# Eight large experts of a two-block transformer: split products on the whole array against unsplit products on four 32-column tiles

## The chip, the core and the metric

The program runs on one core of a Trainium2 chip. The metric is the device time of one execution, in microseconds; the median of three runs is given. The engines are PE (matrix multiply, TensorE), DVE (VectorE), ACT (ScalarE), POOL (GpSimd) and SP, which issues the transfers from memory. PE reads from the on-chip memory of 128 partitions and writes to eight banks of 128 x 512 fp32 accumulators (`psum`).

## The reference

The program computes two transformer blocks on 256 tokens with D = 1024. Two layers of the first block end in a layer of 32 small experts (hidden width 256). The last layer of the second block ends in eight large experts with a hidden width of 2816, and each token goes to two of them. All arithmetic is fp32. Only the last stage matters here:

```python
def swiglu(h, w_gate, w_up, w_down):
    a = jnp.einsum("bsd,df->bsf", h, w_gate)
    u = jnp.einsum("bsd,df->bsf", h, w_up)
    return jnp.einsum("bsf,fd->bsd", jax.nn.silu(a) * u, w_down)

def moe_swiglu(h, router_w, w_gate, w_up, w_down):
    logits = jnp.einsum("bsd,de->bse", h, router_w).astype(jnp.float32)
    top_v, top_i = lax.top_k(logits, TOP_K)
    top_w = jax.nn.softmax(top_v, axis=-1)
    gates = jnp.sum(jax.nn.one_hot(top_i, N_EXPERTS, dtype=jnp.float32) * top_w[..., None], axis=-2)
    y = jnp.zeros(h.shape, jnp.float32)
    for e in range(N_EXPERTS):
        y = y + gates[..., e:e + 1] * swiglu(h, w_gate[e], w_up[e], w_down[e]).astype(jnp.float32)
    return y.astype(h.dtype)
```

On the inputs of the reference the eight experts get 69, 57, 40, 70, 76, 67, 75 and 58 tokens. The kernel computes an expert only for its own tokens, gathered side by side, and reads each weight once.

## The kernel before

**Slots.** `sparse_experts` gathers the tokens by expert into `xg` (1024 rows as 8 k-blocks of 128, one column for each slot). An expert with at most 128 tokens takes the short path, which works on a window of 128 slots from the expert's offset; one with more takes the general path over 256 slots. Each engine reads the expert's count into a register and branches (`by_width`, L2683 and L2684).

**Weights.** An expert has 3 x 11 tiles of 1 MB of weights. SP brings them (128 partitions x 8 KB) into a ring of nine, `weight_ring`, in the order in which PE wants them. A tile is refilled when PE has counted it as used. `SplitExpert` has 33 tiles for an expert and skips 3 places of the ring, so that each expert starts at the same place.

**Split products.** Every weight tile is split into two fp32r parts: ACT copies it to a rounded high part (L2068, `high`), DVE subtracts that from the tile for the low part (L2073, `low`). ACT's copy waits until PE has used the tile that had the buffer before. PE then computes high x high, low x high and high x low (`three_products`, L137 to L139), three matmuls of which each passes 512 weight columns (256 in the last step) through the array, with 128 slots as its stationary operand. The array is used whole, 128 rows x 128 columns.

**Steps.** The hidden width is worked in six steps, five of 512 and one of 256. For each step PE computes gate and up (`first`), ACT takes the Silu of gate (`squash`), DVE multiplies it with up (`combine`), PE turns the result by transposes (`turn`, L2015), ACT and DVE split the turned rows again (L2115, L2119, L2136, L2141), and PE computes the step's share of the down projection (`third`). The turn of a step stands in the middle of the next step's gate, so that ACT and DVE have their time. After the last step the result's rows are copied from two banks by ACT (L2125) and DVE (L2148), turned by PE (L2056) and written to `outT` by DVE (L2152). The first half is copied while PE works at the second half of the last down tile.

**The small experts** (`SmallExperts`, L2317 gate and up, L2348 down, L2338 and L2357 transposes) are another class that the change leaves alone. They use unsplit fp32 products on 64 slots in two column tiles of 64, so that two matmuls share the array; they stand in a loop of several experts a turn, whose general path lies behind each expert and is jumped over by a branch (L2302). An fp32 product is recorded as two loads and two matmuls. Their weights come in rows of 8 KB.

**Order.** Nothing schedules: each engine's instructions stand in the order of the code, SP's loads too, and waits on semaphores tie them together. The eight experts are written out one after the other; the general path is a loop in between.

## Time and profile before

| | |
|---|---|
| median of 3 runs | 2376.32 us (2370.53, 2376.32, 2376.93) |
| the profiled execution | 2376.97 us, its span 2375.2 us |
| PE busy | 2193.2 us, 92% of the span |
| DVE busy | 1452.3 us, 61% |
| ACT busy | 1179.4 us, 50% |
| read from memory | 605.11 MB, 255 GB/s over the span |
| the eight large experts | 1576.7 to 2351.0 us, in the span |
| granted clock of PE | 0.9 or more of full in all 40 slices |

Times within the trace count from the start of the span. The profile lists an instruction's start and duration; matmuls are pipelined, so each lasts longer than the distance to the next, and it is the distance that counts. "idle before <-releaser" is how long the engine stood before an instruction and what it then got. PEq or PEldq is PE's sequencer, which reads the instructions and takes the branches; "issue" is time for which the profile shows no other reason.

### The profile page before, as it was taken

How to read it: one execution, taken by the hardware profiler on the slowest of the kernel's cores; microseconds unless marked ns; L12 is line 12 of the kernel's file. 1: busy time of each engine (PE TensorE's matmuls, PEld its weight loads, DVE VectorE, ACT ScalarE, POOL GpSimd, SP SyncE). 2: the span in 40 equal slices, each digit the busy share in tenths (PEclk: the TensorE clock that was granted, in tenths of full speed). 3: DMA queues.
4: the chain of work that ended last, by engine and by line, in shares of the span. 5: the costliest groups of instructions: out<-in, count | busy, mean ns of one | idle time of the engine just before them, and what ended most of it. 6: DMA issues, size and time to landing. Idle time of an engine off the chain costs nothing.

```text
span 2375.2 us, 35807 instructions
## 1 busy us (share of the span) xinstructions
PE 2193.2 (92%) x13160; PEld 1772.4 (75%) x13160; DVE 1452.3 (61%) x1811; ACT 1179.4 (50%) x1463; POOL 70.2 (3%) x122
## 2 busy tenths in 40 slices
PE   7898988998998889898999989899999999999997
PEld 6774545976654459787998888778788887888886
DVE  5541113565311137964566698468888888888886
ACT  4432222363222234544433455357777777777675
POOL 0100000101000002000000200000000000000000
PEclk9999999999999999999999999999999999999999
DMA  7339998702499976242554633338999999999992
GB/s 261 130 137 419 419 419 298 220 34 92 173 418 419 419 270 184 90 160 89 183 190 144 184 125 125 125 123 319 385 334 389 346 338 390 334 388 349 337 395 107
DMA packets 253801, 609.28 MB, mean 257 GB/s; under 512 B 11216, under 2 KB 103200, under 8 KB 229008
## 3 DMA queue, kind: packets, MB, share of 16 engines
q1 hardware_dynamic: 247776, 590.84, 67.1%
q0 software_dynamic: 5248, 13.25, 2.5%
q8 instruction: 159, 2.61, 0.4%
q10 hardware_dynamic: 560, 2.10, 0.2%
q14 instruction: 58, 0.48, 0.1%
HBM read 605.11 MB, written 1.05 MB: 255 GB/s over the span
## 4 chain that ended last, share of the span: by engine, by line
PE 70%; DVE 12%; DMA 9%; ACT 4%; issue 3%; DVEq 1%; ACTq 0%; SPq 0%; POOLq 0%
PE psum L137 16%; PE psum L139 16%; PE psum L138 16%; DMA weight_ring<-in_moe_w_up_dram 8%; PE psum L2317 7%; PE psum L2348 2%; DVE weight_ring_rounded L116 2%; DVE h_cf L3257 1%; PE psum L936 1%; ACT scores L970 1%; PE psum L2838 1%; ACT weights_high_rounded L2068 1%; PE psum L2357 1%; PE psum L922 1%; PE psum L2015 1%
## 5 line engine op out<-in xcount | busy, mean ns | idle before, releaser
L2073 DVE TENSOR_TENSOR weight_ring_rounded<-weight_ring,weights_high_rounded 128x2048 fp32r<-128x2048 f32 x264 | 603.8, 2291 | 100.0 <-ACT weights_high_rounded L2068 98.9
L2068 ACT ACTIVATE weights_high_rounded<-weight_ring 128x2048 fp32r<-128x2048 f32 x264 | 504.9, 1916 | 149.7 <-PE psum L139 133.5
L2317 PE MATMUL psum<-weight_ring,scores 128*64 128x256 f32 x2048 | 261.3, 397 | 54.0 <-DMA weight_ring<-in_moe_w_up_dram 27.3
L137 PE MATMUL psum<-weights_high_rounded,scores_rounded 128*128 128x512 f32 (+1 forms) x768 | 291.4, 379 | 7.8 <-issue 4.1
L139 PE MATMUL psum<-weights_high_rounded,scores_rounded 128*128 128x512 f32 (+1 forms) x768 | 287.3, 374 | 0.0
L138 PE MATMUL psum<-weight_ring_rounded,scores_rounded 128*128 128x512 f32 (+1 forms) x768 | 286.6, 373 | 0.0
L2317 PEld LDWEIGHTS psum<-weight_ring,scores 128*64 128x64 f32 x2048 | 151.8, 141 | 164.0 <-issue 117.5
L139 PE MATMUL psum<-weights_high_rounded,xT_rounded 128*128 128x512 f32 (+3 forms) x688 | 259.0, 376 | 0.0
L2447 DVE COPY e_outT<-psum 128x512 f32 x64 | 44.3, 692 | 300.2 <-PE psum L2357 300.2
L137 PE MATMUL psum<-xT_high_rounded,weights_high_rounded 128*128 128x256 f32 x768 | 218.0, 284 | 2.2 <-DVE xT_rounded L369 1.4
L139 PE MATMUL psum<-xT_high_rounded,weight_ring_rounded 128*128 128x256 f32 x768 | 217.1, 283 | 0.0
L116 DVE TENSOR_TENSOR weight_ring_rounded<-weight_ring,weights_high_rounded 128x2048 fp32r<-128x2048 f32 (+3 forms) x76 | 159.7, 2113 | 64.9 <-ACT weights_high_rounded L112 64.4
L138 PE MATMUL psum<-xT_rounded,weights_high_rounded 128*128 128x256 f32 x672 | 189.1, 281 | 0.0
L137 PEld LDWEIGHTS psum<-weights_high_rounded,scores_rounded 128*128 128x128 f32 x768 | 145.4, 189 | 35.9 <-DVE weight_ring_rounded L2073 5.9
L139 PEld LDWEIGHTS psum<-weights_high_rounded,scores_rounded 128*128 128x128 f32 x768 | 145.1, 189 | 25.9
L138 PEld LDWEIGHTS psum<-weight_ring_rounded,scores_rounded 128*128 128x128 f32 x768 | 145.4, 189 | 24.9
L112 ACT ACTIVATE weights_high_rounded<-weight_ring 128x2048 fp32r<-128x2048 f32 (+3 forms) x76 | 133.4, 1767 | 48.1 <-PE psum L139 41.3
L139 PEld LDWEIGHTS psum<-weights_high_rounded,xT_rounded 128*128 128x128 f32 x688 | 131.4, 191 | 24.6
L137 PEld LDWEIGHTS psum<-xT_high_rounded,weights_high_rounded 128*128 128x128 f32 x768 | 144.9, 189 | 3.6 <-DVE xT_rounded L369 1.6
L139 PEld LDWEIGHTS psum<-xT_high_rounded,weight_ring_rounded 128*128 128x128 f32 x768 | 144.5, 188 | 0.0
L137 PE MATMUL psum<-weights_high_rounded,xT_rounded 128*128 128x512 f32 x352 | 139.8, 397 | 0.0
L138 PE MATMUL psum<-weight_ring_rounded,xT_rounded 128*128 128x512 f32 x352 | 138.8, 394 | 0.0
(581 smaller groups left out, 3521.0 us busy)
## 6 DMA issues: line engine op xcount, KB each, us to landing
weight_ring<-in_moe_w_gate_dram SPq DMA_DIRECT2D x152, 1024.0 KB, 9.5
weight_ring<-in_moe_w_up_dram SPq DMA_DIRECT2D x152, 1024.0 KB, 10.1
weight_ring<-in_moe_w_down_dram SPq DMA_DIRECT2D x152, 1024.0 KB, 10.3
weight_ring<-in_w_in_dram SPq DMA_DIRECT2D x20, 1024.0 KB, 8.3
weight_ring<-in_ffn_w_gate_dram SPq DMA_DIRECT2D x11, 1024.0 KB, 5.2
weight_ring<-in_ffn_w_up_dram SPq DMA_DIRECT2D x11, 1024.0 KB, 5.3
weight_ring<-in_ffn_w_down_dram SPq DMA_DIRECT2D x11, 1024.0 KB, 4.9
weight_ring<-in_w_out_dram SPq DMA_DIRECT2D x8, 1024.0 KB, 5.0
```

What stands on the lines that cost most here:

```text
L112: self.ring.nc.scalar.activation(self.high, self.whole, ACT.Copy).then_inc(self.ring.high_ready, 1)
L116: self.ring.nc.vector.tensor_tensor(self.low, self.whole, self.high.bitcast(F32), ALU.subtract).then_inc(self.ring.split_ready, 1)
L137: nc.tensor.matmul(out, lh, rh, start=start, stop=False)
L138: nc.tensor.matmul(out, lh, rl, start=False, stop=False)
L139: return nc.tensor.matmul(out, ll, rh, start=False, stop=stop)
L922: last = nc.tensor.transpose(c.psum[:, 4 + g % 2, a * P:(a + 1) * P], S[:, u % 4, place(i), s * P:(s + 1) * P], c.ident[:, :])
L936: last = nc.tensor.matmul(c.psum[:, 6 + u % 2, at:at + P], PT[g % PTS][:, a * P:(a + 1) * P], wide, start=(s == 0), stop=(s == kts[j] - 1))
L2068: self.c.nc.scalar.activation(ring.high(self.s0 + q, 1, SLOT), ring.view(self.p0 + q, 1, SLOT), ACT.Copy).then_inc(ring.high_ready, 1)
L2073: self.c.nc.vector.tensor_tensor(ring.low(self.p0 + q, 1, SLOT), ring.view(self.p0 + q, 1, SLOT), ring.high(self.s0 + q, 1, SLOT).bitcast( ...
L2317: last = self.c.nc.tensor.matmul(psum[at:at + W, x % 2, 0:CH], self.x[:, x % 2, k, :], w[:, k, :], start=(k == 0), stop=(k == k1 - 1), ski ...
L2348: last = nc.tensor.matmul(psum[h * W:(h + 1) * W, 4 + x % 2, :], self.hidden[:, m, :], wt[:, m, h * 512:(h + 1) * 512], start=(m == 0), st ...
L2447: nc.vector.tensor_copy(self.outT[:, :, bass.ds(o, W)].rearrange("p (h j) s -> p j h s", h=2), c.psum[:, 6 + y % 2, :].rearrange("p (j h s ...
```

## The change

`LargeExperts` takes the place of `SplitExpert`. What it does:

- The short path works on 96 slots and is taken up to 96 tokens.
- The hidden width is worked in three steps of 1024, 1024 and 768.
- The weights are not split. A k-block's product (`by_quarters`) puts 32 slots at a time as stationary operand into a tile of 32 columns of the array. The tiles at columns 0, 32 and 64 take slots 0 to 31, 32 to 63 and 64 to 95 and pass the first `main` weight columns (768, or 640 in the last step); the tile at column 96 takes the remaining 256 (or 128) columns for the three groups of slots one after the other, into the same banks on the partitions 96 to 127. Matmuls have at most 512 columns.
- Gate and up come in 4 tiles a step with rows of 4 KB (3 KB in the last step), down in 4, 4 and 3 tiles, with rows of 8 KB in the first two steps, where two hidden rows that follow each other lie side by side. That is 35 tiles an expert, one place of the ring skipped.
- ACT does the window's copy, Silu, the copy of the turned rows and half of the result's; DVE the product and the other half, and three copies to `outT`. The result's rows are turned in the middle of the next expert's first gate.
- The general path (`wide_tensor`, `wide_scalar`, `wide_vector`) reads the weight tiles where they are, with two row groups of 128 slots, and is written out and not a loop.
- The slots' weights are summed in bank 5 and not 3, and DVE clears `rows` once.

The core of the diff, without the unused general path, signals and bookkeeping:

```diff
-class SplitExpert:
...
-                    last = three_products(nc, psum[:, bank + j % 2, 0:cols], (self.xh[:, x, :], self.xl[:, x, :]),
-                                          (high[:, k, :], low[:, k, :]), x == 0, x == KD - 1)
...
-        self.c.nc.scalar.activation(ring.high(self.s0 + q, 1, SLOT), ring.view(self.p0 + q, 1, SLOT), ACT.Copy).then_inc(ring.high_ready, 1)
...
-        self.c.nc.vector.tensor_tensor(ring.low(self.p0 + q, 1, SLOT), ring.view(self.p0 + q, 1, SLOT),
-                                       ring.high(self.s0 + q, 1, SLOT).bitcast(F32), ALU.subtract).then_inc(ring.split_ready, 1)
...
+class LargeExperts:
...
+    W = 96
+    STEPS = ((0, 1024, 768), (1024, 1024, 768), (2048, 768, 640))
+    TILES = 35
...
+    def by_quarters(self, slots, w, bank, main, start, stop):
+
+
+        nc, psum = self.c.nc, self.c.psum
+        rest = w.shape[1] - main
+        for c0, c1 in ((0, 512), (512, main)):
+            for q in range(3):
+                last = nc.tensor.matmul(psum[32 * q:32 * q + 32, bank + c0 // 512, 0:c1 - c0], slots(q), w[:, c0:c1],
+                                        start=start, stop=stop, skip_group_check=True)
+            for q in range(3):
+                if c0 <= q * rest < c0 + 512:
+                    at = q * rest - c0
+                    last = nc.tensor.matmul(psum[96:P, bank + c0 // 512, at:at + rest], slots(q, True), w[:, main:],
+                                            start=start and at == 0, stop=stop, skip_group_check=True)
+        return last
+
+    def first(self, pe, e, name, j, bank, half=None):
+
+        _, width, main = self.STEPS[j]
+        for a in range(4):
+            at = self.tile(e, name, a)
+            self.landed(pe, at, 0)
+            w = self.c.ring.view(at, 2, width)
+            for k in (2 * a, 2 * a + 1):
+                if k == KD // 2 and half is not None:
+                    half()
+                x = self.x[:, e % 2, k, :]
+                last = self.by_quarters(lambda q, rest=False: x[:, 32 * q:32 * q + 32], w[:, k - 2 * a, :], bank, main, k == 0, k == KD - 1)
+            last.then_inc(self.c.ring.used, 1)
...
+    def turn(self, pe, e, j):
+        pe.wait_ge(*self.of(self.rows_made, e, j))
+        if j > 0:
+            pe.wait_ge(*self.of(self.hidden_ready, e, j - 1))
+        elif e > 0:
+            pe.wait_ge(*self.of(self.written, e - 1))
+        for b, rows in self.blocks(j):
+            last = self.c.nc.tensor.transpose(self.c.psum[:, 6 + b // 4, b % 4 * P:(b % 4 + 1) * P], rows, self.c.ident[:, :])
+        last.then_inc(self.turned.sem, 2 if j == 2 else 1)
+
+    def third(self, pe, e, j, spare=0, between=None):
+        pe.wait_ge(*self.of(self.hidden_ready, e, j))
+        hidden = self.hidden[(3 * e + j) % 2].rearrange("p (b s) -> p b s", s=P)
+        tiles = self.parts[f"down{j}"]
+        for a in range(len(tiles)):
+            at = self.tile(e, f"down{j}", a)
+            self.landed(pe, at, 0)
+            w = self.c.ring.view(at, 2, D)
+            for m in range(2):
+                kept = (a == 3) if j < 2 else (a == 2 and m == 1)
+
+                def slots(q, rest=False):
+                    if kept:
+                        return hidden[:, 2 * q + m if j < 2 else q, 96:P]
+                    return hidden[:, 2 * a + m, 32 * q:32 * q + 32]
+                last = self.by_quarters(slots, w[:, m, :], 4, 768, j == 0 and a == 0 and m == 0, j == 2 and a == 2 and m == 1)
+            last.then_inc(self.c.ring.used, 1 + (spare if a == len(tiles) - 1 else 0))
+            if between and a == 0:
+                between()
+
+    def turn_rows(self, pe, e):
+        pe.wait_ge(*self.of(self.rows_act, e))
+        pe.wait_ge(*self.of(self.rows_dve, e))
+        for b in range(6):
+            last = self.c.nc.tensor.transpose(self.c.psum[:, 6 + b // 4, b % 4 * P:(b % 4 + 1) * P], self.rows[:, b * P:(b + 1) * P], self.c.ident[:, :])
+        last.then_inc(self.rows_turned.sem, 1)
+
+    def narrow_tensor(self, pe, e, spare):
+        pe.wait_ge(*self.of(self.windowed, e))
+        if e > 0:
+            pe.wait_ge(*self.of(self.squash_done, e - 1, 2))
+        self.first(pe, e, "gate0", 0, 0, (lambda: self.turn_rows(pe, e - 1)) if e > 0 else None)
+        if e > 0:
+            pe.wait_ge(*self.of(self.rows_made, e - 1, 2))
+        self.first(pe, e, "up0", 0, 2)
+        pe.wait_ge(*self.of(self.squash_done, e, 0))
+        self.first(pe, e, "gate1", 1, 0, lambda: self.turn(pe, e, 0))
+        self.third(pe, e, 0)
+        self.first(pe, e, "up1", 1, 2)
+        pe.wait_ge(*self.of(self.squash_done, e, 1))
+        self.first(pe, e, "gate2", 2, 0, lambda: self.turn(pe, e, 1))
+        self.first(pe, e, "up2", 2, 2)
+        self.third(pe, e, 1, 0, lambda: self.turn(pe, e, 2))
+        self.third(pe, e, 2, spare)
+
+    def narrow_scalar(self, act, e):
+        copy, psum = self.c.nc.scalar.activation, self.c.psum
+        act.drain().then_inc(self.wide_windowed.sem, 1)
+        for j, (_, _, main) in enumerate(self.STEPS):
+            s = 3 * e + j
+            self.done(act, e, f"gate{j}")
+            if s > 0:
+                act.wait_ge(*self.of(self.rows_made, (s - 1) // 3, (s - 1) % 3))
+            copy(self.squashed[:, 0:main], psum[:, 0:2, :].rearrange("p b n -> p (b n)")[:, 0:main], ACT.Silu).then_inc(self.squash_done.sem, 1)
+            act.wait_ge(*self.of(self.turned, e, j))
+            if s > 1:
+                self.done(act, (s - 2) // 3, f"down{(s - 2) % 3}")
+            copy(self.hidden[s % 2][:, 0:main], psum[:, 6:8, :].rearrange("p b n -> p (b n)")[:, 0:main],
+                 ACT.Copy).then_inc(self.hidden_ready.sem, 2 if j == 2 else 1)
+        self.done(act, e, "down2")
+        copy(self.rows[:, 0:512], psum[:, 4, :], ACT.Copy).then_inc(self.rows_act.sem, 1)
+
+    def narrow_vector(self, dve, e, o):
+        nc, psum = self.c.nc, self.c.psum
+        for j, (_, _, main) in enumerate(self.STEPS):
+            s = 3 * e + j
+            self.done(dve, e, f"up{j}")
+            dve.wait_ge(*self.of(self.squash_done, e, j))
+            if s > 0:
+                dve.wait_ge(self.turned.sem, self.of(self.turned, (s - 1) // 3, (s - 1) % 3)[1])
+            nc.vector.tensor_tensor(self.hidden_rows[:, 0:main], self.squashed[:, 0:main], psum[:, 2:4, :].rearrange("p b n -> p (b n)")[:, 0:main],
+                                    ALU.mult).then_inc(self.rows_made.sem, 1)
+        self.done(dve, e, "down2")
+        nc.vector.tensor_copy(self.rows[:, 512:], psum[:, 5, 0:256]).then_inc(self.rows_dve.sem, 1)
+        made = psum[:, 6:8, :].rearrange("p b n -> p (b n)")[:, 0:768]
+        dve.wait_ge(*self.of(self.rows_turned, e))
+        nc.vector.tensor_copy(self.outT[:, 0:6, bass.ds(o, self.W)], made.rearrange("p (k s) -> p k s", k=6)[:, :, 0:self.W])
+        for m in range(2):
+            last = nc.vector.tensor_copy(self.outT[:, 6 + m, bass.ds(o, self.W)].rearrange("p (g s) -> p g s", g=3),
+                                         made.rearrange("p (g m s) -> p m g s", g=3, m=2)[:, m, :, self.W:])
+        last.then_inc(self.written.sem, 1)
...
+    def tensor(self, pe, spare):
+        following = self.load_count(pe, 0)
+        for e in range(self.n):
+            count = following
+            if e + 1 < self.n:
+                following = self.load_count(pe, e + 1)
+            self.by_width(pe, count, lambda: self.narrow_tensor(pe, e, spare), lambda: self.wide_tensor(pe, e, spare))
+        self.turn_rows(pe, self.n - 1)
+
...
-        way = SplitExpert(c, p0, per, chunks, xg, squashed, hidden, outT, landed, used)
...
+        way = LargeExperts(c, p0, n, per, xg, outT, landed, used, cnt_i, off_i)
```

How PE's instructions stand at the start of the first large expert, before. `weight_ring_rounded` are the low parts, `weights_high_rounded` the high parts, `scores_rounded` the window of slots:

```order
L2684 COMPARE_AND_BRANCH
L137 MATMUL psum<-weights_high_rounded,scores_rounded 128x512
L138 MATMUL psum<-weight_ring_rounded,scores_rounded 128x512
L139 MATMUL psum<-weights_high_rounded,scores_rounded 128x512
L137 MATMUL psum<-weights_high_rounded,scores_rounded 128x512
L138 MATMUL psum<-weight_ring_rounded,scores_rounded 128x512
L139 MATMUL psum<-weights_high_rounded,scores_rounded 128x512
```

And now; here `weights_high` is the window of 96 slots, and the shape is that of the output, 32 partitions by columns:

```order
L2216 COMPARE_AND_BRANCH
L2231 MATMUL psum<-weight_ring,weights_high 32x512 x3
L2236 MATMUL psum<-weight_ring,weights_high 32x256 x2
L2231 MATMUL psum<-weight_ring,weights_high 32x256 x3
L2236 MATMUL psum<-weight_ring,weights_high 32x256
L2231 MATMUL psum<-weight_ring,weights_high 32x512 x3
L2236 MATMUL psum<-weight_ring,weights_high 32x256 x2
```

Where three matmuls of the whole array passed 512 columns, nine on 32 columns each now pass 768 columns over each of four tiles, and every fp32 one is a pair in the trace.

At the end of an expert, PE before: the result's transposes, the jump, the general path in a loop, the next expert's count and branch:

```order
L2056 MATMUL psum<-ident,scores 128x128 x8
L2684 UNCONDITIONAL_BRANCH
L2161 UNCONDITIONAL_BRANCH
L2161 ISA
L2165 MATMUL psum<-scores,xT 128x256 x16
L2169 MATMUL psum<-xT_high,scores 128x256 x8
L2161 REGISTER_ALU
L2161 COMPARE_AND_BRANCH
L2686 UNCONDITIONAL_BRANCH
L2683 TENSOR_LOAD e_cnt_i
L2683 ISA x2
L2684 COMPARE_AND_BRANCH
```

The short path ends at `L2684 UNCONDITIONAL_BRANCH`; what lies between it and `L2683 TENSOR_LOAD` isn't executed. And now, on PE at the same place, the jump and the start of the general path:

```order
L2231 MATMUL psum<-weight_ring,xT_high 32x256 x3
L2236 MATMUL psum<-weight_ring,xT_high 32x256
L2216 UNCONDITIONAL_BRANCH
L2363 MATMUL psum<-weight_ring,scores 128x512 x64
L2370 MATMUL psum<-ident,xT 128x128 x16
L2363 MATMUL psum<-weight_ring,scores 128x512 x32
```

The last down products stand right before the jump, with no transposes between. The general path's end and the next expert's start on PE:

```order
L2370 MATMUL psum<-ident,xT 128x128 x12
L2385 MATMUL psum<-weight_ring,xT_high 128x512 x32
L2385 MATMUL psum<-weight_ring,scores 128x512 x24
L2370 MATMUL psum<-ident,xT 128x128 x16
L2218 UNCONDITIONAL_BRANCH
L2213 TENSOR_LOAD e_cnt_i
L2213 ISA x2
L2216 COMPARE_AND_BRANCH
L2231 MATMUL psum<-weight_ring,weights_high 32x512 x3
```

Between the jump (`L2216 UNCONDITIONAL_BRANCH`) and the next expert's count (`L2213 TENSOR_LOAD`) lie some 1,240 instructions of PE, where there were some 100; the result's transposes moved into the next expert.

## Rows read from the trace of the kernel before

**Rows 1.** The page's first line.

```profile
span 2375.2 us, 35807 instructions
```

**Rows 2.** Line L2152: duration min/median/max in ns, first and last start.

```profile
L2152 DVE COPY f_outT<-psum x8: 1217/1218/1226, 1676.3 to 2351.0; 128x1024 f32 x8
```

**Rows 3.** Busy time in stretches: start:end length, each engine (x instructions), granted clock, DMA.

```profile
1676.30:1772.70 96.40, 94.26 (x447) 77.85 (x446) 83.49 (x49) 71.20 (x48) 0.00 (x0) 1.00 0.97 356
1772.70:1869.10 96.40, 95.43 (x453) 79.05 (x452) 85.03 (x49) 68.69 (x47) 0.00 (x0) 1.00 0.98 362
```

**Rows 4.** Waits, 1676:2351: total us, times, longest us.

```profile
ACT weights_high_rounded L2068 <- PE psum L139: 111.8, 166, 2.3
...
PE psum L137 <- DVE weight_ring_rounded L2073: 3.7, 4, 1.2
PE psum L137 <- issue: 3.5, 6, 0.6
PE psum L2056 <- DVE scores L2148: 2.7, 7, 0.4
```

**Rows 5.** Timeline, 2344:2352: start, duration, instruction, xcount.

```profile
2344.36 0.39 PE L137 MATMUL psum<-weights_high_rounded,xT_rounded 128*128 128x512 f32 x1
...
2348.55 0.39 PE L137 MATMUL psum<-weights_high_rounded,xT_rounded 128*128 128x512 f32 x1
...
2349.25 0.60 PE L2056 MATMUL psum<-ident,scores 128*128 128x128 f32 x4
```

**Rows 6.** Groups by form, 1676:2351: total us, mean ns, idle before.

```profile
L2141 DVE TENSOR_TENSOR xT_rounded<-psum,xT_rounded 128x512 fp32r<-128x512 f32 x35 | 23.9, 684 | 0.0
...
L2015 PE MATMUL psum<-ident,xT_high 128*128 128x128 f32 x154 | 23.6, 272 | 0.0
L2119 ACT ACTIVATE xT_rounded<-psum 128x512 fp32r<-128x512 f32 x35 | 21.0, 599 | 44.5 <-PE psum L2015 44.5
```

**Rows 7.** Timeline of PE, small experts, 268:281.

```profile
269.87 1.95 PE L2317 MATMUL psum<-weight_ring,scores 128*64 128x256 f32 x16
271.65 1.89 PE L2348 MATMUL psum<-weight_ring,xT_high 128*64 128x512 f32 x8
276.79 1.95 PE L2317 MATMUL psum<-weight_ring,scores 128*64 128x256 f32 x16 [3.25 <-issue]
```

**Rows 8.** Timeline of PE, small experts, 305:309.

```profile
305.41 1.95 PE L2317 MATMUL psum<-weight_ring,scores 128*64 128x256 f32 x16 [1.11 <-DMA weight_ring<-in_moe_w_up_dram]
307.29 0.50 PE L2338 MATMUL psum<-ident,xT_high 128*128 128x128 f32 x2
307.63 0.60 PE L2357 MATMUL psum<-ident,xT 128*128 128x128 f32 x4
308.16 1.08 PE L2317 MATMUL psum<-weight_ring,scores 128*64 128x256 f32 x8
```

**Rows 9.** Lines L2348 (269:274) and L1573 (whole span), as in group 2.

```profile
L2348 PE MATMUL psum<-weight_ring,xT_high x8: 592/592/593, 271.6 to 272.9; 128*64 128x512 f32 x8
...
L1573 PE MATMUL psum<-c_blocks,weight_ring x128: 275/275/348, 462.2 to 476.4; 128*128 128x128 f32 x128
```

**Rows 10.** Timeline, an attention stage, 499.5:501.

```profile
500.01 0.71 PE L913 MATMUL psum<-c_kvT,c_qT 64*128 64x128 f32 x8
```

**Rows 11.** Line L2302's branches on PE's sequencer: 177:398, and 270:276.

```profile
L2302 PEldq COMPARE_BRANCH  x117: 71/174/5569, 177.2 to 390.1; - x117
...
L2302 PEldq COMPARE_BRANCH  x1: 5314/5314/5314, 270.5 to 270.5; - x1
```

**Rows 12.** Waits in the small experts, 177:398.

```profile
PE psum L2317 <- issue: 17.0, 8, 3.5
```

**Rows 13.** DMA: GB/s in 40 slices and mean of 1676:2351; mean of 200:380.

```profile
GB/s 395 394 395 379 223 365 395 395 393 381 237 381 394 393 393 314 263 391 393 394 384 236 351 396 395 395 379 251 372 392 394 393 382 222 383 393 394 390 282 0
DMA packets 106579, 237.10 MB, mean 351 GB/s; under 512 B 3616, under 2 KB 17952, under 8 KB 106530
...
DMA packets 10442, 75.30 MB, mean 418 GB/s; under 512 B 1142, under 2 KB 1289, under 8 KB 1289
```

**Rows 14.** Timeline of PE at the first large expert, 1581:1583.

```profile
1581.52 0.63 PE L139 MATMUL psum<-weights_high_rounded,scores_rounded 128*128 128x512 f32 x1
```

575 lines of the change are left out of this document (201 added, 374 removed).

## The prediction, made before the changed kernel was timed

> **What bounds the kernel now.** I read the profile in this order. First the page: the profiled execution has a span of 2375.2 us [rows 1]. Only the last stage, the eight large experts, is changed, so the second view is the line whose copy ends an expert: L2152 starts from 1676.3 to 2351.0 [rows 2], seven periods in 674.7 us, 96.4 us for one expert. Third, the busy time in such a period: PE 94.26 and 95.43 us of 96.4, DVE 83.49 and ACT 71.20, the granted clock full, the transfers 0.97 of their engines' time [rows 3]. Two things are nearly full, PE and DMA; the waits of these seven periods tell which waits for which. PE's matmuls waited 3.7 us for a split weight, 3.5 us for their own issue and 2.7 us for DVE at an expert's end, 9.9 us or 1.4 us each, and never for a transfer; ACT waited 111.8 us for PE to give a buffer back [rows 4]. So PE is the bound, and the transfers run at PE's speed behind a full ring.
>
> The period can be rebuilt from its instructions. From the L137 at 2344.36 to the one at 2348.55 are 18 matmuls of 512 columns [rows 5], 0.2328 us each. Gate and up take 5 steps x 8 k-blocks x 2 x 3 products = 240 of 512 columns and 48 of 256 in the last step, down 22 blocks x 2 halves x 3 = 132 of 512. 372 x 0.2328 = 86.6; 48 x 0.1164 = 5.6; 30 transposes at (0.60 - 0.27)/3 = 0.11 us [rows 5, 6] are 3.3; waits 1.4. The sum, 96.9, is 0.5 above the measured 96.4: the method is good to half a per cent.
>
> **The change part by part.** One unsplit fp32 product on 96 slots, spread over four 32-column tiles of PE, takes the place of three fp32r products on 128 slots.
>
> *Products, on the path.* No 32-column tile is in this trace. The nearest rows are the small experts' two 64-column tiles, also unsplit fp32 with weights as the moving operand; a product is two records there. 16 records of 256 columns last 1.95 us and 8 of them 1.08 [rows 7, 8], so 8 records are 0.87 us and a pair, one on each tile, 0.2175. A pair of 512 columns takes (1.89 - 0.59)/3 = 0.43 [rows 7, 9]. That is 0.85 ns a column for two tiles, and a single record on the whole array takes 14.2/127 = 0.112 us for 128 columns, 0.87 ns [rows 9]: the two tiles run at once. In the new code a k-block has 768 columns on each tile: three tiles take the first 768 columns of a step for 32 slots each, the fourth the other 256 for all three groups. If four run at once as two do, a block takes 2 x 0.43 + 2 x 0.2175 = 1.29 us, and 1.29 - 0.2175 = 1.075 in the last gate and up step with 640. An expert has 32 + 22 long blocks and 16 short ones: 69.7 + 17.2 = **86.9 us** against 92.2. The gain is small because a weight column cost 3 x 0.2328/512 = 1.36 ns and costs 1.29/1024 = 1.26 now.
>
> *Rate of issue.* 18 records in a block are one in 71.7 ns, in the short ones 59.7. The densest run here starts eight records in (0.71 - 0.27)/7 = 63 ns each [rows 6, 10]. So long blocks are within what is seen, and short ones could take 18 x 63 = 1.134 us, 16 x 0.06 = 0.9 us more an expert. I take 0 and keep 0.9 for the range.
>
> *Transposes and changes of tiling, on the path.* 17 of hidden rows and 6 of the result, 23 x 0.11 = 2.5 us. Each of four turns now goes from narrow tiles to the whole array and back. From the L2317 at 305.41 to the one at 308.16 are 2.75 us, of which 8 pairs take 1.74 and 6 transposes 0.66 [rows 8]; 0.35 is left for both changes, 4 x 0.35 = 1.4 us. PE's own work is 86.9 + 2.5 + 1.4 = **90.8 us**.
>
> *The jump at an expert's end, on the path.* The general path is written out: 1,241 instructions for PE stand behind each short path and are jumped over, where some 100 in a loop stood. The nearest rows are the small experts' jumps. A branch there took 5.6 us at most and 5.3 at 270.5 [rows 11], after which PE stood for 3.25 us before 276.79 [rows 7]; eight waits of L2317 for issue took 17.0 us, 2.1 on average, 3.5 at most [rows 12]. The bounds are 0.3 (the short jump of before costs no more) and 5.3 (nothing queued covers it). I take 3.5: every new jump lands beyond anything that stands near it, as the longest of those did. The clock holds over such a pause, since the run at 276.79 lasts 1.95 us like the one at 269.87 [rows 7]. The period becomes 90.8 + 3.5 = **94.3 us**.
>
> The Trainium skill, "Runtime: NRT & Kernel Launch", Instruction fetch mechanics, says that blocks of 256 instructions are fetched ahead in sequence only, that a taken branch out of the window held has to wait for a fetch, and that running across a block's end is mostly hidden. By it each of the seven jumps costs a fetch and the longer short path nothing; the branches of 5.3 and 5.6 us agree.
>
> *ACT and DVE, off the path.* 33 high copies (L2068) and 33 low parts (L2073) an expert go. The latter ended 3.7 us of PE's waits in seven periods [rows 4], so they are worth 0.5 us each, which the new sum already leaves out. The new waits of PE are covered: at a turn it waits for a Silu by ACT and a product by DVE of 768 columns, some 0.9 and 1.0 us by the 0.599 and 0.684 us for 512 [rows 6], behind four blocks of the next gate, 5.2 us; the last turn has one down tile, 2.6 us. The result's two copies lie behind four blocks of the next expert's gate, with nothing but the jump ahead of them on ACT and DVE.
>
> *Transfers, off the path.* 33 tiles of 1.0486 MB, 34.6 MB, become 35 tiles with rows of twice the length and the same bytes. They streamed at 395 GB/s where nothing held them, 87.6 us an expert, and at 418 in the small experts, 82.8 us [rows 13]. Both are below 90.8. At under 367 GB/s they would be the bound at 94.3. I take 0.
>
> *Ends.* The first expert starts at half clock in both (0.63 us a matmul still at 1581.52, where it is 0.39 later [rows 5, 14]) and has no jump ahead of it: 90.8 - 96.4 = -5.6. At the end the result is copied only after the last product, where half of it was copied earlier: +0.5.
>
> **Sum.** 7 x (94.3 - 96.4) = -14.7; -5.6; +0.5: **-19.8 us**. The profiled execution took 2376.97 us, 1.8 more than its span, and the median is 2376.32, so the difference holds for either: 2376.3 - 19.8 = **2356.5 us**. A measurement of this kernel can tell 0.3%, 7.1 us, from no change; this is 0.8%.
>
> **The rivals.**
> A: the jump is hidden, the period 91.1, the sum 7 x (-5.3) - 5.6 + 0.5 = -42: 2334 us. For it: with a mean of 2.1 and a maximum of 3.5, some of the eight waits are short [rows 12]. Against it: the target is far in every one of the new jumps.
> B, the slower side: four tiles don't reach the rate of two. Its place is every k-block, its price a share of 8 x 86.9 = 695 us: 1% is 7.0 us. The gain is gone at 2.8%, 36 ns in a block or 2 ns a record; at 5% it gives 2356.5 + 34.8 = 2391, at 8% 2412. For it: a block goes over the tiles in runs of unequal lengths (three of 512, two of 256, three of 256, one of 256), so one tile may stand while another catches up. Against it: the second tile of [rows 7] costs nothing.
> C: issue or tiles bound it outright. At 112 ns a record a block is 2.02 us, an expert's products 141 us, the kernel 2356.5 + 8 x 54.5 = 2792 us; if two tiles ran at a time, 2356.5 + 695 = 3051. Against it are the 63 ns of [rows 10].
> D: the transfers decide. At the mean of seven periods, 351 GB/s [rows 13], an expert takes 98.6 us, 2376.3 + 8 x 2.2 = 2394. That mean holds the idle times of a full ring and is a lower bound of the rate, so it gets little.
> That the new short path isn't taken can't be: the reference's inputs give the eight experts 40 to 76 tokens.
>
> A figure of a page speaks against the change at the place of B and C. The Trainium skill, "TensorE: Matmul & The Clock Gate", Measured speedup vs the span model, gives 2.38 for three column tiles, 0.79 of full. By it, an estimate, the products take 110 us and the kernel 2356.5 + 8 x 23 = 2541, a case inside C; that the second tile of [rows 7] is free speaks against it, and no row shows a third.
>
> **How the numbers follow.** The forecast with its own spread (2345 to 2369) 0.40; A (2328 to 2345) 0.15; no difference, by B at 2 to 4% or D in part (2369 to 2383.5) 0.13; B or D in full (2383.5 to 2415) 0.19; C and B above 8% 0.13. So faster 0.55, same 0.13, slower 0.32. The range goes from 2328, A with no cost of the jump at all, to 2415, B at 8% with the 0.9 us of the short blocks in part; C is left out.
>
> **What the profile after would show.** A block every 1.29 us and records down to some 60 ns apart; the copy to the result every 94.3 us; one wait of PE for issue of some 3.5 us an expert, beside a branch of some 5 us on its sequencer; no wait of PE for a transfer; ACT and DVE under 15% busy. A block of over 1.33 us would prove B, records no closer than 75 ns C, waits for the ring D, and each makes the forecast wrong.

## The result: slower by half a per cent

| | before | changed |
|---|---|---|
| median of 18 runs | 2377.39 us (2365.88 to 2380.51) | 2388.94 us (2379.79 to 2394.51) |
| the profiled execution, its span | 2376.97, 2375.2 us | 2387.54, 2385.8 us |
| ratio to before | | 1.0055, 95% interval 1.0043 to 1.0068 |

The changed kernel is 11.6 us slower, where 19.8 us less was forecast. The page's first lines, of the changed kernel:

```profile
span 2385.8 us, 48106 instructions
...
PE 2175.3 (91%) x19824; PEld 1645.6 (69%) x19824; DVE 810.9 (34%) x1482; ACT 668.4 (28%) x1151; POOL 70.3 (3%) x122
```

PE is busy 18 us less than before over the span and the span is 10.6 us longer. So PE's own work fell, as meant, and the time is in pauses. First, one k-block. The timeline of PE at the first expert (start, duration, instruction, count of records):

```profile
1577.58 0.60 PE L2231 MATMUL psum<-weight_ring,weights_high 128*32 128x512 f32 x3
1577.60 0.59 PE L2236 MATMUL psum<-weight_ring,weights_high 128*32 128x256 f32 x2
1578.01 0.60 PE L2231 MATMUL psum<-weight_ring,weights_high 128*32 128x512 f32 x3
...
1578.87 0.60 PE L2231 MATMUL psum<-weight_ring,weights_high 128*32 128x512 f32 x3
```

From 1577.58 to 1578.87, one block of 18 records, are 1.29 us: the figure of the forecast to the last digit, and records stand 71.7 ns apart with four tiles at work. Second, the distance between experts, read from a copy at each expert's end. L2344 is the changed kernel's, L2148 the one that does the same before (both: duration min/median/max in ns, first and last start):

```profile
L2344 DVE COPY weights_high<-psum x8: 424/425/425, 1666.5 to 2359.3; 128x256 f32<-128x256 f32 x8
```

```profile
L2148 DVE COPY scores<-psum x8: 684/684/692, 1673.1 to 2349.5; 128x512 f32<-128x512 f32 x8
```

Seven periods are 692.8 us in the changed kernel, 98.97 each, and 676.4 before, 96.6. (The forecast said 94.3, with PE's own work at 90.8.) The waits from 1576 to 2351 (total us, times, longest us; compare [rows 4]):

```profile
ACT xT_high L2328 <- PE psum L2268: 414.9, 24, 25.0
...
PE psum L2231 <- issue: 39.6, 7, 6.0
```

Nothing waits for a transfer, no wait of PE for ACT or DVE is left, and ACT sits 415 us idle for want of hidden rows. PE waits for one thing, its own issue, seven times and 39.6 us. Here is the first, on PE's timeline:

```profile
1666.06 0.38 PE L2236 MATMUL psum<-weight_ring,xT_high 128*32 128x256 f32 x1
1671.64 1.07 PE L2231 MATMUL psum<-weight_ring,weights_high 128*32 128x512 f32 x3 [5.20 <-issue]
...
1672.47 1.10 PE L2231 MATMUL psum<-weight_ring,weights_high 128*32 128x512 f32 x3
...
1674.17 1.10 PE L2231 MATMUL psum<-weight_ring,weights_high 128*32 128x512 f32 x3
...
1676.67 0.61 PE L2231 MATMUL psum<-weight_ring,weights_high 128*32 128x512 f32 x3
...
1677.96 0.61 PE L2231 MATMUL psum<-weight_ring,weights_high 128*32 128x512 f32 x3
```

The last product of the first expert starts at 1666.06, the second expert's first at 1671.64: PE stood for 5.20 us. And what follows has another speed. Records of 512 columns last 1.10 us instead of 0.60, from 1672.47 to 1674.17 are 1.70 us for what took 0.86 from 1578.01 to 1578.87, and only from 1676.67 to 1677.96 is a block 1.29 us again. The stretch table shows the same for the second jump: the granted clock is 1.00 over the whole expert and 0.71 over the 11.7 us around the jump, that is 2.4 GHz and a part at 1.2 GHz:

```profile
1677.00:1764.80 87.80, 87.80 (x1246) 60.24 (x1239) 3.82 (x6) 4.66 (x6) 0.00 (x0) 1.00 0.97 355
1764.80:1776.50 11.70, 5.68 (x53) 2.78 (x49) 0.42 (x1) 1.45 (x2) 0.00 (x0) 0.71 0.79 309
```

All seven starts are alike: gaps of 5.6 to 6.4 us from start to start, and half clock until 4.1 to 5.0 us behind the new expert's first product. At the first jump the clock fell at 1669.77, in the pause, and came back at 1676.60:

```profile
1671.64:1676.60 4.96, 4.96 (x36) 2.47 (x40) 0.00 (x0) 0.00 (x0) 0.00 (x0) 0.50 0.70 282
```

The sequencer's own rows show where the time goes: the branch L2216 at 1664.7 took 6007 ns, and behind it come the register load of the next count (307 ns) and what belongs to it:

```profile
L2216 PEldq COMPARE_BRANCH  x2: 83/3045/6007, 1664.7 to 1671.4; - x2
...
L2213 PEldq TENSOR_LOAD <-e_cnt_i x8: 298/307/318, 1574.2 to 2166.5; - x8
L2213 PEldq FUSED_REGOPS  x8: 146/152/155, 1574.6 to 2166.8; - x8
```

What the branch waits for stands in the trace too. The DMA queue q8 carries PE's code in packets of 16 KB: from 1576 to 2351 there are 93 of them here, and 69 in the run of experiment 9, in which only PE has fewer instructions. From 1664.9 to 1671 the trace has one such packet. This is the window 1668.2:1669.3 (packets, MB, share):

```profile
q8 instruction: 1, 0.02, 5.2%
```

It starts at 1668.29, 3.63 us behind the branch, takes 0.92 us, and the branch ends 1.46 us after it has landed. All seven jumps are like this: the packet starts 3.5 to 4.4 us behind the branch, and the branch ends 1.4 to 1.5 us behind its landing. So is the trace of before: all 23 of PE's branches of over 1 us end 1.35 to 1.55 us behind the landing of such a packet, the one at 270.5 among them, whose packet starts 2.8 us behind it. A far jump is a wait for a piece of code. Most of it passes before the piece starts to move, and here the weights may be in its way: the eighth jump, behind the last expert, comes when no weights are under way, its packet starts after 0.91 us, and its branch takes 3.3 us in all. The stretch from the branch to the packet at the first jump and at the eighth (the last two numbers are the DMA's share and GB/s):

```profile
1664.66:1668.29 3.63, 1.78 (x27) 0.97 (x19) 0.42 (x1) 1.09 (x2) 0.00 (x0) 1.00 1.01 395
2357.48:2358.39 0.91, 0.91 (x18) 0.67 (x14) 0.00 (x0) 0.00 (x0) 0.00 (x0) 1.00 0.06 18
```

That the transfers hold the packet up fits these rows; no run changes the transfers at a jump to show it.

The sum is then 10.6 us for the profiled pair: the first expert's copy comes 6.6 us earlier (1666.5 for 1673.1), seven periods are 16.4 us longer, and from the last such copy to the end of the span are 26.5 us for 25.7.

### The profile page after: what moved, and what is told of

It is laid out like the page before. It is cut to its first block, busy times and chain, and to the rows that moved or that the text cites. A ratio compares the mean times of both kernels' runs of the same rounds, so it can differ in the third digit from the quotient of the medians.

```text
span 2385.8 us, 48106 instructions
## 1 busy us (share of the span) xinstructions
PE 2175.3 (91%) x19824; PEld 1645.6 (69%) x19824; DVE 810.9 (34%) x1482; ACT 668.4 (28%) x1151; POOL 70.3 (3%) x122
## 4 chain that ended last, share of the span: by engine, by line
PE 71%; DVE 12%; DMA 8%; issue 4%; ACT 4%; DVEq 1%; ACTq 0%; SPq 0%; POOLq 0%
PE psum L2231 18%; PE psum L2236 12%; PE psum L1977 7%; DMA weight_ring<-in_moe_w_up_dram 7%; PE psum L137 6%; PE psum L139 6%; PE psum L138 6%; PE psum L2008 3%; DVE weight_ring_rounded L116 2%; DVE h_cf L3181 1%; PE psum L936 1%; ACT scores L970 1%; PE psum L2017 1%; PE psum L2762 1%; PE psum L2268 1%
## 5 line engine op out<-in xcount | busy, mean ns | idle before, releaser
L2231 PE MATMUL psum<-weight_ring,weights_high 128*32 128x512 f32 (+2 forms) x4608 | 491.1, 480 | 39.6 <-issue 39.6
L2236 PE MATMUL psum<-weight_ring,weights_high 128*32 128x256 f32 (+1 forms) x2304 | 458.4, 353 | 0.0
L2236 PEld LDWEIGHTS psum<-weight_ring,weights_high 128*32 128x32 f32 x2304 | 246.2, 112 | 58.3 <-issue 7.0
L2231 PEld LDWEIGHTS psum<-weight_ring,weights_high 128*32 128x32 f32 x4608 | 188.4, 112 | 136.5 <-issue 90.9
L2236 PE MATMUL psum<-weight_ring,xT_high 128*32 128x256 f32 x1056 | 232.2, 379 | 0.0
L2231 PE MATMUL psum<-weight_ring,xT_high 128*32 128x256 f32 (+1 forms) x2112 | 231.5, 486 | 0.0
L2341 DVE TENSOR_TENSOR xT<-xT,psum 128x768 f32<-128x768 f32 (+1 forms) x24 | 21.8, 910 | 509.4 <-PE psum L2236 371.5
L2107 DVE COPY e_outT<-psum 128x512 f32 x64 | 44.3, 692 | 299.1 <-PE psum L2017 299.1
L2236 PEld LDWEIGHTS psum<-weight_ring,xT_high 128*32 128x32 f32 x1056 | 114.8, 110 | 37.3
L137 PE MATMUL psum<-weights_high_rounded,xT_high_rounded 128*128 128x512 f32 (+3 forms) x336 | 124.3, 370 | 14.3 <-DVE weight_ring_rounded L116 6.4
L138 PEld LDWEIGHTS psum<-xT_rounded,weights_high_rounded 128*128 128x128 f32 x672 | 126.5, 188 | 0.5
L138 PE MATMUL psum<-weight_ring_rounded,xT_high_rounded 128*128 128x512 f32 (+3 forms) x336 | 122.4, 364 | 0.0
```

The lines of the kernel that those rows point to most:

```text
L137: nc.tensor.matmul(out, lh, rh, start=start, stop=False)
L138: nc.tensor.matmul(out, lh, rl, start=False, stop=False)
L2107: nc.vector.tensor_copy(self.outT[:, :, bass.ds(o, W)].rearrange("p (h j) s -> p j h s", h=2), c.psum[:, 6 + y % 2, :].rearrange("p (j h s ...
L2231: last = nc.tensor.matmul(psum[32 * q:32 * q + 32, bank + c0 // 512, 0:c1 - c0], slots(q), w[:, c0:c1], start=start, stop=stop, skip_group ...
L2236: last = nc.tensor.matmul(psum[96:P, bank + c0 // 512, at:at + rest], slots(q, True), w[:, main:], start=start and at == 0, stop=stop, ski ...
```

## The experiments

Times are medians, ratios are to the kernel before in runs on the same chip.

**1. PE's branches away.** PE's stream runs the eight short paths in a row:

```diff
-            self.by_width(pe, count, lambda: self.narrow_tensor(pe, e, spare), lambda: self.wide_tensor(pe, e, spare))
+            self.narrow_tensor(pe, e, spare)
```

> The changed kernel with PE's general path and its branches left out: PE runs the short path of all eight experts in a row; ACT and DVE keep theirs. It computes the reference only while no expert has more than 96 tokens, as here. Theory J (the jump): each of the seven jumps over the general path costs PE 5.9 us of standing still (gaps of 5.6 to 6.4 us in the trace of the changed kernel) and then about 2.1 us at half clock. Without them the distance between two experts' first matmuls falls from 99.0 to 90.9 us and the time from 2388.9 to about 2332 us; no stretch at half clock stands at an expert's start. Rival T (the transfers): PE's pause hides that the ring would be empty; then PE's waits change from issue to DMA, the distance stays above 95 us and the time above 2360. Rival W (the wait at the boundary is for ACT's window or the count's register, not for the code): the gaps shrink only by what the branch itself takes, 0.1 us, and the time stays near 2389.

2333.92 us, ratio 0.9826 (0.9809 to 0.9842). The end-of-expert copy:

```profile
L2344 DVE COPY weights_high<-psum x8: 424/424/425, 1672.4 to 2308.8; 128x256 f32<-128x256 f32 x8
```

636.4/7 = 90.91 us an expert, where theory J said 90.9. PE's waits for issue are gone. 98.97 - 90.91 = 8.06 us is what one jump costs. The rivals T (transfers) and W (a wait for ACT or for the count's register) fall: no other wait takes the jump's place, and the counts are still loaded here.

**2. The far jump put into the kernel before.** The loop of PE's general path is written out; it isn't run here either.

```diff
-        with pe.Fori(0, 2 * self.chunks) as h:
+        for h in range(2 * self.chunks):
```

> The kernel before with one edit: the loop of PE's general path is written out 22 times, some 2,100 instructions between the experts that are never run here. Theory J: the far jump costs this kernel as much as the changed one, 5.9 us of gap and up to 2.1 us of half clock, less the 1.4 us that PE waits there already: 7 x 5 to 8 = +35 to +56 us, 2412 to 2433. Rival (the jump only hurts where the short path is four times as dense in instructions, since fetches then come late): no change, 2377.

2433.93 us, ratio 1.0248 (1.0231 to 1.0265), +59.8 us, a little above the +35 to +56 that J gave. L2152 as in [rows 2], and PE's timeline at the first jump:

```profile
L2152 DVE COPY f_outT<-psum x8: 1217/1219/1226, 1676.3 to 2406.2; 128x1024 f32 x8
...
1681.05 0.76 PE L137 MATMUL psum<-weights_high_rounded,scores_rounded 128*128 128x512 f32 x1 [6.51 <-issue]
1681.61 0.63 PE L138 MATMUL psum<-weight_ring_rounded,scores_rounded 128*128 128x512 f32 x1
```

(2406.2 - 1676.3)/7 = 104.3 us for 96.4. PE stands 6.51 us and then works at 0.63 us a matmul, the half clock. So the cost doesn't belong to the four tiles, the unsplit weights or the short path's many instructions; the one part of the change that is never run makes the kernel before slower too. One of the seven gaps is 12 us long, which is why the upper end was passed; it ends 1.5 us behind the landing of a second 16 KB packet.

**3. to 6. How far is far?** PE's general path was cut to its first matmuls, or stood twice. None of these instructions is run here.

```diff
-            self.by_width(pe, count, lambda: self.narrow_tensor(pe, e, spare), lambda: self.wide_tensor(pe, e, spare))
+            self.by_width(pe, count, lambda: self.narrow_tensor(pe, e, spare), lambda: self.cut_general(pe, e, spare))
...
+    def cut_general(self, pe, e, spare):
+        self.wide_first(pe, e, "gate0", 0)
```

> The changed kernel with PE's general path cut to its first 32 matmuls, some 130 instructions (the rest of it is left out; it isn't run with these inputs). It tells the branch from its distance. Theory J (distance, code that isn't there yet): a target some 130 instructions on has been fetched with what runs, so the gap falls under 1.5 us, the clock holds, the distance between experts is 91 to 92.5 us and the time 2332 to 2345. Rival (a taken branch as such, with the register load behind it, empties the sequencer and costs the same at any distance): gap 5.9 us as before and 2389.

> The changed kernel with PE's general path cut to 64 matmuls, some 256 instructions (the rest is left out; it isn't run). 130 instructions cost nothing at any of the seven jumps, 510 cost 5.5 to 6.1 us at all of them. Theory J (the target is held only if it lies in the piece of code that is already there behind the running one): here it depends on where each jump lies in its piece, so a part of the seven jumps pays: distances between experts of 91 or of 99 us, mixed, and 2345 to 2375. Rival (the cost grows smoothly with the distance): all seven gaps alike at 1 to 4 us.

> The changed kernel with PE's general path cut to 128 matmuls, some 510 instructions (the rest is left out; it isn't run). The distance of the jump lies between the 130 of the last cut, which cost nothing, and the 1,241 of the changed kernel. If a target is only there when the running code's fetches have reached it, and they reach some 256 to 512 instructions on, part of the jumps find it and part don't: a distance between experts of 91 to 99 us and a time between 2332 and 2389, near 2360. If anything beyond 256 is lost: gaps of 5.9 us at all seven and 2389. If 512 are still held: 2332.

> The changed kernel with PE's general path standing there twice, some 2,480 instructions (it isn't run). Theory J, a target that isn't held is fetched at one price whatever the distance: gaps of 5.6 to 6.4 us and 2389 us as with 1,241. Rival (the code in between is fetched through, 2.5 us for 256 instructions): gaps of over 20 us and above 2480.

| instructions jumped over, about | time | ratio, interval | an expert |
|---|---|---|---|
| none (experiment 1) | 2333.92 | 0.9826 (0.9809 to 0.9842) | 90.91 |
| 130 | 2331.28 | 0.9822 (0.9806 to 0.9839) | 90.91 |
| 256 | 2343.32 | 0.985 (0.983 to 0.987) | 92.7 |
| 510 | 2391.94 | 1.0072 (1.0051 to 1.0093) | 99.2 |
| 1,241 (the changed kernel) | 2388.94 | 1.0055 (1.0043 to 1.0068) | 98.97 |
| 2,480 | 2410.89 | 1.0147 (1.012 to 1.0175) | 101.7 |

With 130 a branch takes 397 ns at most, and the period is that without any branch (branches of L2216 on PE's sequencer, then the copy):

```profile
L2216 PEldq COMPARE_BRANCH  x16: 71/127/397, 1571.4 to 2300.2; - x16
...
L2344 DVE COPY weights_high<-psum x8: 424/425/425, 1665.6 to 2302.0; 128x256 f32<-128x256 f32 x8
```

So a taken branch with a register load behind it costs nothing here, only its distance does; and no 16 KB packet starts while such a branch lasts. With 510 the branches take up to 6.55 us, and all seven gaps are there, 5.5 to 6.1 us:

```profile
L2216 PEldq COMPARE_BRANCH  x16: 81/1686/6553, 1574.0 to 2357.6; - x16
...
L2344 DVE COPY weights_high<-psum x8: 424/425/425, 1664.9 to 2359.4; 128x256 f32<-128x256 f32 x8
```

My expectation of a half-way time was wrong: at 510 every jump already pays in full. It is at 256 that the case is mixed, and there not as I had written it either (91 or 99 us, and 2345 at least) but in small parts: no branch over 2.2 us, and six pauses of 6.7 us together, of which one, the longest, is followed by half clock:

```profile
L2216 PEldq COMPARE_BRANCH  x16: 71/192/2175, 1573.3 to 2314.4; - x16
...
PE psum L2231 <- issue: 6.7, 6, 2.1
...
L2344 DVE COPY weights_high<-psum x8: 423/425/425, 1667.5 to 2316.2; 128x256 f32<-128x256 f32 x8
```

The q8 packets show why. At three of the jumps the packet had started 0.3 to 1.4 us before the branch, which so paid only for the rest of it (1.0 to 2.2 us); at the other four the branch cost nothing (0.3 to 0.4 us), and PE paused some 6 us later, until 1.3 to 1.5 us behind the landing of the next packet. So at 256 a jump pays for the part of a fetch that is still open. The doubled path also missed its forecast. Its first gaps are the ones of the changed kernel (5.50 us here), as J says and against a fetch of everything in between; but four of its jumps have a second pause a few instructions on, of 2.6 to 4.1 us, and at another the gap is 10.9 us:

```profile
1970.99 0.38 PE L2236 MATMUL psum<-weight_ring,xT_high 128*32 128x256 f32 x1
1976.87 1.88 PE L2231 MATMUL psum<-weight_ring,weights_high 128*32 128x512 f32 x3 [5.50 <-issue]
1981.77 1.06 PE L2231 MATMUL psum<-weight_ring,weights_high 128*32 128x512 f32 x2 [3.02 <-issue]
...
L2344 DVE COPY weights_high<-psum x8: 424/425/425, 1670.5 to 2382.4; 128x256 f32<-128x256 f32 x8
```

At 1976.87 three matmuls of the new expert are started, and the next wait until 1981.77. The target had come and the code behind it hadn't: a second 16 KB packet starts at 1979.32, lands at 1980.39, and PE goes on 1.4 us later. The second pauses and the gap of 10.9 us all end so, 1.35 to 1.53 us behind the second packet's landing. Which jumps have one may depend on where the target lies in its packet; no run shows that. The changed kernel has none such, the one with 510 has one.

**7. The register load.** All counts are read before the first expert:

```diff
-        following = self.load_count(pe, 0)
-        for e in range(self.n):
-            count = following
-            if e + 1 < self.n:
-                following = self.load_count(pe, e + 1)
+        counts = [self.load_count(pe, e) for e in range(self.n)]
+        for e, count in enumerate(counts):
```

> The changed kernel with all eight counts read into PE's registers ahead of the first expert, so that behind a jump stands only the branch. In the trace of the changed kernel the register load and its checks take 0.7 of the 5.9 us of a gap. Theory J: gaps shorter by 0.7 us each, 7 x 0.7 = -5 us, 2384. Rival (the load is what makes the gap): gaps under 2 us and 2345.

2389.49 us, ratio 1.0061 (1.0041 to 1.0082): no gain. The gaps are shorter, 4.8 to 5.0 us in six of seven, and an expert takes 685.1/7 = 97.87 us, 1.1 less. From the branch's end to the first product are 0.31 us where there were 0.97, so the load is 0.65 us of it; the branches are shorter too, 6.08 us on average for 6.57. What this gave, the stage's start took, where the first copy comes 6.9 us later: eight loads stand ahead of the first product, which now begins at 1580.30 behind a pause of 2.64 us. It begins at half clock as well, but the clock had fallen at 1576.0, before the pause, so that part needn't be the loads'.

```profile
1574.79 2.87 PE L2699 MATMUL psum<-f_w,f_outT 128*128 128x1 f32 x18
1580.30 1.07 PE L2231 MATMUL psum<-weight_ring,weights_high 128*32 128x512 f32 x3 [2.64 <-issue]
...
L2344 DVE COPY weights_high<-psum x8: 424/424/425, 1673.4 to 2358.5; 128x256 f32<-128x256 f32 x8
```

So the load is under 1 us of a jump's 8, and the rival falls.

**8. What the queue covers.** The small experts' jump, on which the forecast was built, has a branch as long as the new one (5.3 us, [rows 11]) and a pause of only 3.25 us. Between the branch at 270.5 and the last record before the pause 18 matmul records start there; behind the branch at 1664.66 of the changed kernel 22 start. So what is queued is about the same in number, and not in time. Eight useless matmuls of 512 columns were put right ahead of the jump, in a kernel with the jumps and in one without (the last experiment's):

```diff
         self.third(pe, e, 2, spare)
+        for k in range(KD):
+            self.c.nc.tensor.matmul(self.c.psum[:, 2, :], self.xg[:, 0, 0:P], self.xg[:, k, 0:512], start=True, stop=True, skip_group_check=True)
```

> The changed kernel with eight more matmuls at each expert's end, right ahead of the jump (window columns by 512 of the gathered slots, fp32 on the whole array, into a bank that nobody reads then): 16 records of 0.427 us, 6.8 us more work for PE in each of eight experts, of no use for the result. Theory Q (PE has some 18 to 22 matmul records queued when its sequencer takes the branch; what they take in time is the cover of the fetch, here 1.5 us since a short record takes 71 ns, in the small experts up to 3 us): the queued records now last 7 us, so the gap of 5.9 falls under 1 us and the clock holds. Per expert +6.8 - 5.5 - 2.2 = about -1: the time stays at 2382 to 2392 in spite of 55 us more work. Rival (the fetch starts only when PE has run dry): +55, 2444.

> The kernel with one branch for all experts and the same eight useless matmuls at each expert's end. No jump is there to be covered, so both theories say that the whole 6.8 us of each expert is paid: 2335 + 55 = 2390 us. Were it less, the extra work would be hidden by something else (a wait at the boundary that the queue hides), and the reading of the other run would fall.

With the jumps 2396.98 us, ratio 1.0081 (1.0055 to 1.0106); without 2387.48, ratio 1.0052 (1.0036 to 1.0069). By the ratios the same work costs 0.26% (6 us, give or take as much) in the changed kernel, 1.0055 without it, and 2.2% (51 us) in the one without jumps, 0.9836. At the first jump:

```profile
1672.39 0.39 PE L2231 MATMUL psum<-weight_ring,xT_high 128*32 128x256 f32 x3
...
1672.78 7.13 PE L2316 MATMUL psum<-e_xg 128*128 128x512 f32 x16
1679.84 0.63 PE L2231 MATMUL psum<-weight_ring,weights_high 128*32 128x512 f32 x3
...
L2216 PEldq COMPARE_BRANCH  x2: 83/2904/5726, 1672.8 to 1679.2; - x2
...
L2346 DVE COPY weights_high<-psum x8: 424/424/425, 1672.9 to 2365.4; 128x256 f32<-128x256 f32 x8
```

The branch begins at 1672.8, when the first of the 16 long records starts, and ends 5.7 us later; the 16 last 7.1 us, and the next expert starts at 1679.84 with no pause and at full clock. Five of seven periods are 98.1 us, those of the kernel without jumps:

```profile
L2346 DVE COPY weights_high<-psum x8: 424/424/425, 1667.9 to 2354.7; 128x256 f32<-128x256 f32 x8
```

(2354.7 - 1667.9)/7 = 98.11. Theory Q holds: the fetch starts with the branch, runs beside whatever PE has queued, and only the rest is paid. It is 5 us over my 2382 to 2392, since two jumps had the second pause of the doubled path (2.3 and 3.6 us from start to start), and since the 16 records take 7.2 and not 6.8 us.

**9. Is the fourth tile free?** Its columns are left out, so the output isn't the reference's.

```diff
             for q in range(3):
-                if c0 <= q * rest < c0 + 512:
+                if False:
```

> The changed kernel without the fourth tile's matmuls (the last 256 or 128 weight columns of each step are left out of gate, up and down, so the output isn't the reference's); 12 records a block in place of 18. If the tiles run at once without a price, a block still takes 1.29 us and 1.075 in the last step, the time is 2389 less nothing. If the fourth tile costs something, this is faster: each per cent of the products is 7 us. The instructions are a third fewer, so the far jump keeps its 5.6 to 6.4 us if it is a fetch.

2380.71 us, ratio 1.0018 (1.0005 to 1.0031), 8.2 us less than the changed kernel. But the blocks didn't move. Two views of the last gate-and-up step with windows of different length:

```profile
1739.55 6.64 PE L2231 MATMUL psum<-weight_ring,weights_high 128*32 128x512 f32 x72
...
1738.47 8.79 PE L2231 MATMUL psum<-weight_ring,weights_high 128*32 128x512 f32 x96
```

24 records more are 8.79 - 6.64 = 2.15 us, so 12, a block, take 1.075; the changed kernel takes 1.08 there with 18. A fourth tile at work costs nothing. The 8 us are in the jumps: 3.9 to 5.5 us from start to start instead of the 5.6 to 6.4 that I had expected to stay, since the 21 records in the queue now last 2.7 us and not 1.8 (a block's 12 records stand 107 ns apart, not 72). Two of the seven have a second pause.

**10. How near the transfers are.** From the kernel with one branch, the last tile of each gate and up isn't multiplied, so the output isn't the reference's:

```diff
+            if a == 3:
+                pe.drain().then_inc(self.c.ring.used, 1)
+                continue
```

> The kernel with one branch for all experts, without the last two of the eight k-blocks of gate and up (left out, so the output isn't the reference's; the tiles are loaded all the same). PE's own work falls by 8 x 1.29 + 4 x 1.075 = 14.6 to 76.3 us an expert, so the transfers become the bound and show their own period: 34.6 MB at the 418 GB/s of the small experts would be 82.8 us, at the 395 of before 87.6, at 376 (the mean now) 92.0. Expected 84 to 87, a time of about 2285, and waits of PE for weights; it tells how far the transfers were from deciding at 90.9.

2278.98 us, ratio 0.958 (0.9555 to 0.9606). PE now waits for weights, and the transfers run without a break (the copy L2347 here is the end-of-expert one; the last line is the mean rate from 1676 to 2240):

```profile
L2347 DVE COPY weights_high<-psum x8: 424/424/425, 1656.8 to 2250.7; 128x256 f32<-128x256 f32 x8
...
PE psum L2231 <- DMA weight_ring<-in_moe_w_gate_dram: 20.1, 12, 2.4
...
DMA packets 56044, 229.60 MB, mean 407 GB/s; under 512 B 3718, under 2 KB 3718, under 8 KB 48846
```

593.9/7 = 84.8 us an expert is the transfers' own period, at 407 GB/s. Rival D's mean rate of 351 GB/s was the ring's idling, as the forecast said. At 90.91 PE is still the bound, with 6 us to spare.

**11. One branch for all eight.** DVE makes the largest count; PE branches once.

```diff
+        most = pe.value_load(self.cnt[0:1, self.n:self.n + 1], min_val=0, max_val=TOK)
+        with pe.If(most < self.W + 1):
+            for e in range(self.n):
+                self.narrow_tensor(pe, e, spare)
+        with pe.Else():
+            for e in range(self.n):
+                self.by_width(pe, self.load_count(pe, e), lambda: self.narrow_tensor(pe, e, spare), lambda: self.wide_tensor(pe, e, spare))
```

> The changed kernel with one branch on PE for all experts: DVE makes the largest of the eight counts, PE runs eight short paths in a row if it is at most 96, and else reads each expert's count and branches as in the changed kernel. All inputs are computed rightly. Theory J: one far jump is left, at the end of the stage, over all of the second copy; it costs some 6 us there and the seven others' 8.1 each are gone: 2332 + 6 = 2338 us, faster than both kernels. Rival T: above 2360, with waits for transfers.

2334.88 us, ratio 0.9836 (0.9819 to 0.9852), where 2338 was expected. It does all that the changed kernel does, is 1.6% faster than before and, by the ratios, 2.2% faster than the change. The one jump left, over all of the second copy, shows before the result's last transposes:

```profile
L2344 DVE COPY weights_high<-psum x8: 424/425/425, 1669.3 to 2305.7; 128x256 f32<-128x256 f32 x8
...
2307.82 0.84 PE L2295 MATMUL psum<-ident,weights_high 128*128 128x128 f32 x6 [2.20 <-issue]
```

From start to start the gap is 2.58 us, where it is 1.07 without a jump (experiment 1); it costs some 1.5 us, not 6, since PE must wait for the copied rows in any case.

## The prediction against this, step by step

**PE's own work: right.** A block 1.29 us (measured 1.29), 1.075 in the last step (1.08), 90.8 us an expert (90.91). Rival B, four tiles short of two, and C, issue as a bound, are out: 72 ns a record with four tiles, 60 in the last step, and a fourth tile that costs nothing. The figure of 2.38 for three column tiles in the Trainium skill, "TensorE: Matmul & The Clock Gate", Measured speedup vs the span model, isn't seen here; the measurement decides.

**Transfers, ACT and DVE: right.** No wait for either in the changed kernel. 84.8 us were measured where the forecast had 82.8 to 87.6. Relief of ACT and DVE gave no more than PE's few waits for them, 6.4 us in the seven periods of [rows 4].

**The jump: wrong, and this is the step that failed.** The term was 3.5 us a jump with bounds of 0.3 and 5.3; it is 8.06 (98.97 - 90.91), outside its own bounds. Three things were missed, each with its number:
- The price was taken from the pause of the small experts (3.25 us, at most 3.5), when what carries over is the branch's duration (5.3 to 5.6, [rows 11]), less what PE has queued. Even that grew here, to 6.0 to 6.8, as the 16 KB packet started later. Some 20 matmul records cover a part of it. They lasted 3.0 us there, from 270.5 to the pause, and 1.8 us here, from 1664.66 to 1666.44, because the change makes records of 72 ns. The change itself took away the cover that the row showed.
- The upper bound was the branch alone. The branches took up to 6.8 us here, and the next count's load and checks stand behind six of the seven, 1.0 us from the branch's end to the first product (0.3 at the seventh, which has no load). The first jump adds up: 6.0 + 1.0 - 1.8 = 5.2 us.
- "The clock holds over such a pause" was read at 3.25 us and used for 3.5. Over 5.6 to 6.4 us it doesn't: it is at 1.2 GHz behind every one of the seven, for 4.1 to 5.0 us, half of which is lost: the rest of the 8.06, some 2.2 us.

7 x (8.06 - 3.5) = 31.9 us. The forecast's -19.8 with it is +12.1, and the measured difference of the medians is +11.6. The sum needs no other correction beyond the profiled pair's first expert, which came 6.6 and not 5.6 us earlier: the clock was full at its start in the changed kernel and half in the one before. That varies between kernels whose code up to there is the same: experiment 1 started at half clock, experiment 11 at full. The clock was half at that start in 10 of the 14 traces.

**Rival A**, the jump hidden, 2334 us, is what the kernel is when it has no far jump: 2331 to 2335. So the sum was right and its case wrong. The slower side that came true wasn't among the rivals: B had the right size (its +15 us stand at 5%) and the wrong place. The forecast asked what price to give to the jump and treated it as a term with one answer; a cost for which the nearest rows show 0.1 to 5.6 us on a sequencer, in a change that gains 5 us an expert, should have been the slower rival, with its point of decision: without a price of the jump the forecast's sum is -44.3 us, so from 44.3/7 = 6.3 us a jump on the kernel is slower than before. The bound of 5.3 kept me from seeing it.

**The rule of the page** on instruction fetch (the Trainium skill, "Runtime: NRT & Kernel Launch", Instruction fetch mechanics) is borne out in kind: a jump over 130 instructions is free, over 510 it isn't, and each of the seven waits for one 16 KB packet. It says nothing of the price, and the forecast's "each costs a fetch" left that open.

## What to carry to other kernels

Code that is never run isn't free when a jump has to go over it: put it where one jump serves for all, or make it a short loop. Price a jump by the branch's own duration on the sequencer, taken where the transfers run as in the stage in question (3.3 us in the changed kernel without them, 6.0 to 6.8 beside them), less what the engine has queued at that moment, in time and not in count, and add the cold clock if the rest is long. And when a change makes instructions shorter, everything that their queue used to hide comes out.
